# A two-block transformer kernel in fp32: the last step of four layer norms moves from GpSimd to VectorE

## The chip, the cores and the metric

The kernel runs on one core of a Trainium2 chip. Its time is the device time of one execution in microseconds; what is told is the median over runs. The engines are named as in the profile: PE is TensorE's matmul side and PEld its weight loads, DVE is VectorE, ACT is ScalarE, POOL is GpSimd, SP is SyncE, which here only issues DMAs.

## What is computed

The input is one sequence of 256 tokens of width 1024. A first block (two hybrid layers) yields `x`. The second block, in which the change lies, runs two layers over `x` (the latent stream) and a context stream `ctx` of 256 tokens:

```python
for i in range(2):
    last = i == 1
    h, hc = x * (1 + sc1) + sh1, ctx * (1 + sc1c) + sh1c
    y, yc = retention_mixer(h, hc, ...) if i == 0 else neighbourhood_mixer(h, hc, ...)
    x = layer_norm(ALPHA * x + g1 * y, ln_g[i, 0], ln_b[i, 0])
    h = x * (1 + sc2) + sh2
    x = layer_norm(ALPHA * x + g2 * sq_relu_mlp(h), ln_g[i, 1], ln_b[i, 1])
    if not last:
        ctx = layer_norm(ALPHA * ctx + g1c * yc, ln_g[i, 0], ln_b[i, 0])
        ctx = layer_norm(ALPHA * ctx + g2c * sq_relu_mlp(ctx * (1 + sc2c) + sh2c), ln_g[i, 1], ln_b[i, 1])
# sq_relu_mlp(h) = square(relu(h @ w1)) @ w2, with w1 1024 x 4096 and w2 4096 x 1024
```

## The kernel before, in words

Every engine has its own instruction list, and semaphores alone order them. All large products are made in three passes: a weight block is split by ACT into a rounded part `w_hi` (`split_hi`, L412) and by DVE into the rest `w_lo` (`split_lo`, L420), and `three` (L431 to L433) multiplies hi by hi, hi by lo and lo by hi. The weights come in units of 128x2048 fp32. SP fetches a unit into one of four `raw` slots (L368) and waits for the slot's last split; the split parts have two slots, so ACT splits unit n+2 once PE has begun unit n+1. PE takes the units in order.

Tokens lie in four tiles of 128: tiles 0 and 1 are the context (`xc`), tiles 2 and 3 the latent stream (`xs`); `x_of(t)` names tile t. `ALL` is all four, `LAT` the last two. Lines 1688 to 1724 (`dve_ahead`, `dve_half`, `dve_normal`) build ALPHA*x plus the gated result, its statistics, and the normalised tile `y`. PE transposes `y`, ACT applies the next stage's scale and shift, and DVE writes the low part `zt_lo` (L1654, semaphore `zT`), on which the next product starts. The residual stream itself is not needed for that product. It is brought up to date apart from it: `pool_gains2` loads the norm's gain and bias, broadcast over the partitions, into `gn2` (L1811; the profile calls it gn), and `pool_stream` makes x = y * gain + bias for each tile on POOL (L1819, L1822) and counts `zs_new`.

That happens three times: after the retention mixer (ALL, at the start of the first MLP), after the first MLP (ALL, at the start of the neighbourhood stage) and after the neighbourhood mixer (LAT, at the start of the second MLP). The norm after the second MLP is made in `dve_final`.

In the MLP the steps are `up` and `down` over chunks of 512 hidden columns, in the order up 0, up 1, down 0, up 2, down 1 and so on, each in two halves j of one unit. For a half of `up`, ACT makes the relu from PSUM (L2213), DVE the square (L2239, tile `hm`), ACT the rounded part `hh_hi` (L984), ACT and DVE split the next unit (L412, L420), and DVE makes `hh_lo` (L2245, semaphore `hh`). Behind the first `up` DVE waits for `zs_new` and clears `y` with one memset per tile (L2259), since `y` collects the `down` products (L1844). `gate_b` is made from `mod` (L1663) in the same stretch.

In the neighbourhood stage `nv` lies over `y` and `nq` over `gn2`, so ACT waits for `zs_new` before it writes `nv` (L984); SP waits for it before the first bias windows (`nb_windows`, L2330), and POOL before it clears `nb` (L2311).

PE has no work in the norms: `pe_keep` (L790) issues matmuls there whose results nobody reads.

Of the kernel before, what the change touches and what calls it, by code (L numbers as in the profile page):

```python
# [23 lines left out]
ALU = mybir.AluOpType  # L24
# [184 lines left out]
def build(nc, a, out):  # L209

    with ExitStack() as ctx:
        held = {}

        def on(name):
            if name not in held:
                held[name] = ctx.enter_context(nc.semaphore(name))
            return held[name]
# [83 lines left out]
        y = sc("y", [2 * NT, D])  # L301
# [1504 lines left out]
                    on("pow_out"), pool.gives("pow_out"))  # L1806

        def pool_gains2(pool, l, m):
            pool.eng.wait_ge(on("zs_new"), pool.given("zs_new"))
            for j, v in enumerate(("ln_g_2", "ln_b_2")):  # L1810
                pool.eng.dma_start(gn2[:, j, :], a[v][l, m].partition_broadcast(P)).then_inc(  # L1811
                    on("gn2_in"), pool.gives("gn2_in", 16))

        def pool_stream(pool, tiles):

            pool.eng.wait_ge(on("gn2_in"), pool.takes("gn2_in", 32))
            pool.eng.wait_ge(on("zT"), pool.takes("zT", len(tiles)))
            for t in tiles:
                G.tensor_tensor(x_of(t), y[:, t, :], gn2[:, 0, :], ALU.mult).then_inc(  # L1819
                    on("p_step"), pool.gives("p_step"))  # L1820
                pool.eng.wait_ge(on("p_step"), pool.given("p_step"))
                G.tensor_tensor(x_of(t), x_of(t), gn2[:, 1, :], ALU.add).then_inc(  # L1822
                    on("zs_new"), pool.gives("zs_new"))

        def down_unit(pe, h_hi_, h_lo_, tiles, banks, ready=None):
            hi, lo = unit_slot(pe)
# [400 lines left out]
        def dve_mlp(dve, tiles):  # L2227
            n_tok = len(tiles) * P
            streams = sorted({stream_of(t) for t in tiles})

            def step(what, b, c):
                if c is last_down:
                    return
                for j in range(2):
                    if what == "up":
                        for f in range(2):
                            dve.eng.wait_ge(on("relu"), dve.takes("relu"))
                            r2 = hm[:, 2 * j + f, 0:n_tok]
                            V.tensor_tensor(r2, r2, ps[2 * j + f][:, 0:n_tok], ALU.mult).then_inc(  # L2239
                                on("hm"), dve.gives("hm"))  # L2240
                        dve.eng.wait_ge(on("hm"), dve.given("hm"))
                        split_lo(dve)
                        for f in range(2):
                            dve.eng.wait_ge(on("hh_hi"), dve.takes("hh_hi"))
                            V.tensor_tensor(hh_lo[:, b, 2 * j + f, 0:n_tok], hm[:, 2 * j + f, 0:n_tok],  # L2245
                                                    hh_hi[:, b, 2 * j + f, 0:n_tok].bitcast(F32), ALU.subtract).then_inc(
                                                        on("hh"), dve.gives("hh"))
                    else:
                        dve.eng.wait_ge(on("y_add"), dve.given("y_add"))
                        dve_add(dve, j, tiles, down_banks(j, tiles))  # L2250
                        split_lo(dve)
                        if j == 0 and dve.loop is None:
                            dve.eng.wait_ge(on("y_add"), dve.given("y_add"))
                            dve.eng.wait_ge(on("gate_b"), dve.takes("gate_b", 2 * len(streams)))
                            dve_ahead(dve, 0, tiles)
                if what == "up" and dve.loop is None and c == 0:
                    dve.eng.wait_ge(on("zs_new"), dve.takes("zs_new", len(tiles)))
                    for t in tiles:
                        V.memset(y[:, t, :], 0.0).then_inc(on("v_step"), dve.gives("v_step"))  # L2259
                    dve.eng.wait_ge(on("v_step"), dve.given("v_step"))  # L2260

            mlp_program(dve, f"mlp{len(tiles)}", step)
            dve.eng.wait_ge(on("y_add"), dve.given("y_add"))

        def dve_final(dve):
# [2 lines left out]
            dve_half(dve, 0, 3, 5, "ahead")  # L2268
            dve_half(dve, 1, 2, 6, "added")
            dve_half(dve, 1, 3, 7, "added")  # L2270
            dve.eng.wait_ge(on("gn2_in"), dve.takes("gn2_in", 128))
            for t in LAT:
                dve.eng.wait_ge(on("pow_out"), dve.takes("pow_out"))
                o = 32 * (t % 2)
# [32 lines left out]
                nb_windows(sp, f, (2, 3))  # L2307

        def pool_nat(pool):
            pool.eng.wait_ge(on("zs_new"), pool.given("zs_new"))  # L2310
            G.memset(nb[:, 0:SEQ], 0.0).then_inc(on("p_step"), pool.gives("p_step"))  # L2311
            pool.eng.wait_ge(on("p_step"), pool.given("p_step"))
            for f in range(NF):
# [176 lines left out]
        def dve_nat(dve):  # L2490
            split_lo(dve)
            split_lo(dve)
            split_lo(dve)
            dve.eng.wait_ge(on("zs_new"), dve.takes("zs_new", len(ALL)))
            for f in range(NF):
                split_lo(dve)
                dve.eng.wait_ge(on("nqk_ps"), dve.takes("nqk_ps"))
# [92 lines left out]
        def _(eng):  # L2590
# [24 lines left out]
            for m in range(2):  # L2615
                pool_powers(pool, ALL)
                pool_gains2(pool, 0, m)
                pool_stream(pool, ALL)
            pool_nat(pool)
            pool_powers(pool, LAT)  # L2620
            pool_gains2(pool, 1, 0)
            pool_stream(pool, LAT)
            pool_gains2(pool, 1, 1)
            pool_powers(pool, LAT)

# [102 lines left out]
```

## Time and profile before

| | |
|---|---|
| median of 3 runs | 2115.38 us (2114.42 to 2117.17) |
| profiled execution, its own time | 2118.92 us |
| span of the profile | 2116.9 us |
| PE busy | 2045.9 us (97%) |
| DVE busy | 1272.1 us (60%) |
| ACT busy | 876.3 us (41%) |
| POOL busy | 184.3 us (9%) |
| mean granted clock of TensorE | 0.995 |

The busy times are of one profiled execution. The span runs from its first to its last instruction, and its own time is some 2 us longer. A busy PE is not a PE at its peak, so what matters is where PE waits, and for whom. The granted clock is 1.0 at 2.4 GHz and 0.5 at 1.2 GHz.

### The profile page before, as it was taken

Reading aid. Unit: us, or ns where it says so; the run is one execution under the profiler, and the core shown is the slowest. Engines: PE = TensorE matmul, PEld = TensorE weight load, DVE = VectorE, ACT = ScalarE, POOL = GpSimd, SP = SyncE. Lnnn points to the kernel's source line nnn. Section 1 sums busy time; section 2 is a strip of 40 time slices with the busy share of each in tenths; the row PEclk is TensorE's granted clock in tenths of the full one; section 3 lists DMA queues with packets and bytes.
Section 4 is the critical chain, followed back from the end, with each engine's and each line's share of the span. In section 5 each row is a group of like instructions: output and inputs, shape, how many; then the busy total and the mean of one; then the engine's idle time right before and its main releaser. Section 6 shows DMA issues by size and latency. Waiting matters only on the chain.

```text
span 2116.9 us, 31361 instructions
## 1 busy us (share of the span) xinstructions
PE 2045.9 (97%) x12185; PEld 1672.0 (79%) x12185; DVE 1272.1 (60%) x2047; ACT 876.3 (41%) x1459; POOL 184.3 (9%) x175
## 2 busy tenths in 40 slices
PE   8999999999999999999999999999999999789997
PEld 7776899887768998877777778788888787567996
DVE  5656677476567773744444378634445823766667
ACT  5533566354335654422222224323322433755452
POOL 2020200000200000000000004000000420302000
PEclk9999999999999999999999999999999999999999
DMA  8477665644876655322222222332333262535662
GB/s 247 160 268 250 183 178 178 193 126 159 281 256 198 175 183 165 128 79 80 64 95 59 100 60 80 100 100 85 93 99 99 80 146 86 76 93 158 187 187 85
DMA packets 327156, 297.45 MB, mean 141 GB/s; under 512 B 35030, under 2 KB 248354, under 8 KB 326928
## 3 DMA queue, kind: packets, MB, share of 16 engines
q1 hardware_dynamic: 322960, 283.22, 44.7%
q0 software_dynamic: 4096, 12.84, 1.8%
q8 instruction: 70, 1.15, 0.2%
q14 instruction: 30, 0.25, 0.0%
HBM read 294.97 MB, written 1.05 MB: 140 GB/s over the span
## 4 chain that ended last, share of the span: by engine, by line
PE 78%; DVE 13%; issue 3%; ACT 3%; DMA 1%; DVEq 0%; POOL 0%; SPq 0%; ACTq 0%; POOLq 0%
PE ps L431 22%; PE ps L433 21%; PE ps L432 21%; DVE w_lo L420 4%; PE ps L1931 2%; PE ps L499 2%; PE ps L790 1%; DVE npr L2509 1%; DVE hid L1551 1%; PE ps L696 1%; PE ps L2376 1%; PE ps L704 1%; DVE qkv L1222 1%; PE ps L706 1%; PE ps L1912 1%
## 5 line engine op out<-in xcount | busy, mean ns | idle before, releaser
L420 DVE TENSOR_TENSOR w_lo<-raw,w_hi 128x1024 fp32r<-128x1024 f32 x428 | 525.4, 1270 | 354.7 <-ACT w_hi L412 354.5
L412 ACT ACTIVATE w_hi<-raw 128x1024 fp32r<-128x1024 f32 x428 | 428.6, 1051 | 554.3 <-PE ps L431 468.1
L431 PE MATMUL ps<-zt_hi,w_hi 128*128 128x512 f32 (+1 forms) x816 | 276.6, 339 | 4.5 <-issue 1.4
L433 PE MATMUL ps<-zt_hi,w_lo 128*128 128x512 f32 (+1 forms) x816 | 274.9, 337 | 0.0
L432 PE MATMUL ps<-zt_lo,w_hi 128*128 128x512 f32 (+1 forms) x816 | 274.9, 337 | 0.0
L431 PE MATMUL ps<-xt_hi,w_hi 128*128 128x256 f32 x896 | 255.6, 285 | 12.3 <-DVE w_lo L420 10.9
L432 PE MATMUL ps<-xt_lo,w_hi 128*128 128x256 f32 x896 | 252.0, 281 | 0.0
L433 PE MATMUL ps<-xt_hi,w_lo 128*128 128x256 f32 x896 | 251.9, 281 | 0.0
L431 PEld LDWEIGHTS ps<-xt_hi,w_hi 128*128 128x128 f32 x896 | 169.6, 189 | 20.3 <-DVE w_lo L420 11.6
L431 PEld LDWEIGHTS ps<-zt_hi,w_hi 128*128 128x128 f32 x816 | 154.1, 189 | 24.9 <-issue 3.7
L432 PEld LDWEIGHTS ps<-xt_lo,w_hi 128*128 128x128 f32 x896 | 169.8, 189 | 0.0
L433 PEld LDWEIGHTS ps<-xt_hi,w_lo 128*128 128x128 f32 x896 | 169.6, 189 | 0.0
L433 PEld LDWEIGHTS ps<-zt_hi,w_lo 128*128 128x128 f32 x816 | 154.9, 190 | 18.1
L432 PEld LDWEIGHTS ps<-zt_lo,w_hi 128*128 128x128 f32 x816 | 154.1, 189 | 18.4 <-issue 0.2
L431 PE MATMUL ps<-w_hi,hh_hi 128*128 128x512 f32 x384 | 149.9, 390 | 1.7 <-DVE w_lo L420 1.7
L432 PE MATMUL ps<-w_lo,hh_hi 128*128 128x512 f32 x384 | 150.8, 393 | 0.0
L433 PE MATMUL ps<-w_hi,hh_lo 128*128 128x512 f32 x384 | 150.7, 392 | 0.0
L431 PE MATMUL ps<-w_hi,zt_hi 128*128 128x512 f32 x320 | 127.9, 400 | 1.8 <-DVE w_lo L420 1.8
L433 PE MATMUL ps<-w_hi,zt_lo 128*128 128x512 f32 x320 | 126.9, 397 | 0.0
L432 PE MATMUL ps<-w_lo,zt_hi 128*128 128x512 f32 x320 | 126.7, 396 | 0.0
L1844 DVE TENSOR_TENSOR y<-y,ps 128x512 f32<-128x512 f32 x108 | 71.9, 684 | 85.9 <-PE ps L433 85.9
L1551 DVE SCALAR_TENSOR_TENSOR hid<-ps,par,hid 128x254 f32<-128x254 f32 (+1 forms) x176 | 76.9, 478 | 59.8 <-ACT hid L1174 53.8
(382 smaller groups left out, 3424.7 us busy)
## 6 DMA issues: line engine op xcount, KB each, us to landing
raw<-in_mlp_w SPq DMA_DIRECT2D x128, 512.0 KB, 4.6
raw<-in_ada_w SPq DMA_DIRECT2D x96, 512.0 KB, 5.2
raw<-in_w_up SPq DMA_DIRECT2D x88, 512.0 KB, 5.1
raw<-in_w_in SPq DMA_DIRECT2D x56, 512.0 KB, 4.9
raw<-in_ret_w_in SPq DMA_DIRECT2D x48, 512.0 KB, 4.5
raw<-in_w_down SPq DMA_DIRECT2D x44, 512.0 KB, 4.0
raw<-in_nat_w_in SPq DMA_DIRECT2D x24, 512.0 KB, 5.0
raw<-in_w_out SPq DMA_DIRECT2D x16, 512.0 KB, 7.3
```

Source lines behind the costliest of these rows:

```text
L412: nc.scalar.activation(w_hi[:, t, w], raw[:, s, w], ACT.Copy).then_inc(on("w_hi"), act.gives("w_hi"))
L420: ins = nc.vector.tensor_tensor(w_lo[:, t, w], raw[:, s, w], w_hi[:, t, w].bitcast(F32), ALU.subtract)
L431: first = nc.tensor.matmul(out_ap, l_hi, r_hi, start=start, stop=False)
L432: nc.tensor.matmul(out_ap, l_hi, r_lo, start=False, stop=False)
L433: return first, nc.tensor.matmul(out_ap, l_lo, r_hi, start=False, stop=stop)
L499: ins = T.matmul(ps[5][32 * k:32 * k + 32, :], cs[:, 4 * j + k, 22 - 2 * g:54 - 2 * g], raw[:, s, 512 * k:512 * k + 512], start=g == j == ...
L696: ins = T.matmul(ps[2 + t][:, hs(h)], m_lev[n % 2][:, t, hs(h)], x_inv[:, t, hs(h)], start=True, stop=True)
L704: T.matmul(ps[t][:, hs(h)], xt_inv[:, t, hs(h)], dec_y[:, t, hs(h)], start=True, stop=True)
L706: ins = T.matmul(ps[2 + t][:, hs(h)], dec_y[:, t, hs(h)], xt_inv[:, t, hs(h)], start=True, stop=True)
L1551: V.scalar_tensor_tensor(dst[:, d:SEQ], src[:, 0:SEQ - d], w, dst[:, d:SEQ], ALU.mult, ALU.add).then_inc(on(sem), dve.gives(sem))
L1844: V.tensor_tensor(yt, yt, ps[banks[n]][:, :], ALU.add).then_inc(on("y_add"), dve.gives("y_add"))
L1931: ins = T.matmul(ps[4 + t][:, :], s_, rv[:, v, :], start=n == 0, stop=n == len(keys) - 1)
```

## The change

The two instructions per tile that bring the stream up to date move from POOL to DVE. In the MLPs they stand in the first `up` step, half of the tiles behind each half j; in the neighbourhood stage all four tiles stand behind DVE's second split of `dve_nat`. The products of a call come first, then one wait, then the sums. The loads of `gn2` stay on POOL, with the same condition in constants. Waits for `zs_new` on DVE become waits for its own count.

```diff
         def pool_gains2(pool, l, m):
-            pool.eng.wait_ge(on("zs_new"), pool.given("zs_new"))
+            pool.eng.wait_ge(on("zs_new"), (0, len(ALL), 2 * len(ALL), 2 * len(ALL) + len(LAT))[2 * l + m])
...
-        def pool_stream(pool, tiles):
-
-            pool.eng.wait_ge(on("gn2_in"), pool.takes("gn2_in", 32))
-            pool.eng.wait_ge(on("zT"), pool.takes("zT", len(tiles)))
+        def dve_stream(dve, tiles):
+
             for t in tiles:
-                G.tensor_tensor(x_of(t), y[:, t, :], gn2[:, 0, :], ALU.mult).then_inc(
-                    on("p_step"), pool.gives("p_step"))
-                pool.eng.wait_ge(on("p_step"), pool.given("p_step"))
-                G.tensor_tensor(x_of(t), x_of(t), gn2[:, 1, :], ALU.add).then_inc(
-                    on("zs_new"), pool.gives("zs_new"))
+                V.tensor_tensor(x_of(t), y[:, t, :], gn2[:, 0, :], ALU.mult).then_inc(
+                    on("v_step"), dve.gives("v_step"))
+            dve.eng.wait_ge(on("v_step"), dve.given("v_step"))
+            for t in tiles:
+                V.tensor_tensor(x_of(t), x_of(t), gn2[:, 1, :], ALU.add).then_inc(
+                    on("zs_new"), dve.gives("zs_new"))
...
@@ dve_mlp, behind hh_lo of half j of an up step
+                        if dve.loop is None and c == 0:
+                            if j == 0:
+                                dve.eng.wait_ge(on("gn2_in"), dve.takes("gn2_in", 32))
+                            dve_stream(dve, tiles[j * len(tiles) // 2:(j + 1) * len(tiles) // 2])
...
                 if what == "up" and dve.loop is None and c == 0:
-                    dve.eng.wait_ge(on("zs_new"), dve.takes("zs_new", len(tiles)))
+                    dve.eng.wait_ge(on("zs_new"), dve.given("zs_new"))
...
@@ dve_final
-            dve.eng.wait_ge(on("gn2_in"), dve.takes("gn2_in", 128))
+            dve.eng.wait_ge(on("gn2_in"), dve.takes("gn2_in", 32))
...
@@ pool_nat
-            pool.eng.wait_ge(on("zs_new"), pool.given("zs_new"))
+            pool.eng.wait_ge(on("zs_new"), 2 * len(ALL))
...
         def dve_nat(dve):
             split_lo(dve)
             split_lo(dve)
+            dve.eng.wait_ge(on("gn2_in"), dve.takes("gn2_in", 32))
+            dve_stream(dve, ALL)
             split_lo(dve)
-            dve.eng.wait_ge(on("zs_new"), dve.takes("zs_new", len(ALL)))
...
@@ POOL's program
             for m in range(2):
                 pool_powers(pool, ALL)
                 pool_gains2(pool, 0, m)
-                pool_stream(pool, ALL)
             pool_nat(pool)
             pool_powers(pool, LAT)
             pool_gains2(pool, 1, 0)
-            pool_stream(pool, LAT)
             pool_gains2(pool, 1, 1)
```

## Rows read from the trace of the kernel before

**Rows 1.** The page: busy time by engine, and the chain that ended last.

```profile
PE 2045.9 (97%) x12185; PEld 1672.0 (79%) x12185; DVE 1272.1 (60%) x2047; ACT 876.3 (41%) x1459; POOL 184.3 (9%) x175
PE 78%; DVE 13%; issue 3%; ACT 3%; DMA 1%; DVEq 0%; POOL 0%; SPq 0%; ACTq 0%; POOLq 0%
```

**Rows 2.** Timeline of POOL: start, length, instruction, idle before it and its releaser.

```profile
1304.26 2.40 POOL L1819 TENSOR_TENSOR xc<-y,gn 128x1024 f32<-128x1024 f32 x1 [7.44 <-DVE zt_lo L1654]
1324.87 2.71 POOL L1822 TENSOR_TENSOR xs<-xs,gn 128x1024 f32<-128x1024 f32 x1
...
1696.79 2.42 POOL L1822 TENSOR_TENSOR xs<-xs,gn 128x1024 f32<-128x1024 f32 x1
...
1931.18 2.40 POOL L1822 TENSOR_TENSOR xs<-xs,gn 128x1024 f32<-128x1024 f32 x1
```

**Rows 3.** Timeline of DVE in the first MLP's first steps, pairs merged (x2).

```profile
1317.22 5.33 DVE L420 TENSOR_TENSOR w_lo<-raw,w_hi 128x1024 fp32r<-128x1024 f32 x2 [3.12 <-ACT w_hi L412]
1322.46 5.66 DVE L2245 TENSOR_TENSOR hh_lo<-hm,hh_hi 128x512 fp32r<-128x512 f32 x2
1333.32 1.29 DVE L2245 TENSOR_TENSOR hh_lo<-hm,hh_hi 128x512 fp32r<-128x512 f32 x2
1334.77 0.91 DVE L2259 MEMSET y<- 128x1024 f32 x1 [0.16 <-issue]
...
1340.47 1.28 DVE L2239 TENSOR_TENSOR hm<-hm,ps 128x512 f32<-128x512 f32 x2 [1.57 <-ACT hm L2213]
1343.40 2.36 DVE L420 TENSOR_TENSOR w_lo<-raw,w_hi 128x1024 fp32r<-128x1024 f32 x2 [1.65 <-ACT w_hi L412]
```

**Rows 4.** Timelines of DVE, ACT and PE in the second MLP's first steps.

```profile
1931.19 4.60 DVE L420 TENSOR_TENSOR w_lo<-raw,w_hi 128x1024 fp32r<-128x1024 f32 x2 [1.97 <-ACT w_hi L412]
...
1944.04 0.75 DVE L2239 TENSOR_TENSOR hm<-hm,ps 128x256 f32<-128x256 f32 x2 [0.23 <-DVE y L2259]
1946.23 2.36 DVE L420 TENSOR_TENSOR w_lo<-raw,w_hi 128x1024 fp32r<-128x1024 f32 x2 [1.44 <-ACT w_hi L412]
...
1945.15 1.99 ACT L412 ACTIVATE w_hi<-raw 128x1024 fp32r<-128x1024 f32 x2
...
1935.85 0.39 PE L431 MATMUL ps<-zt_hi,w_hi 128*128 128x256 f32 x1 [0.59 <-DVE w_lo L420]
1948.72 0.50 PE L431 MATMUL ps<-w_hi,hh_hi 128*128 128x512 f32 x1 [1.71 <-DVE w_lo L420]
```

**Rows 5.** Timeline of PE in the first MLP: a unit's last matmul, two units' first.

```profile
1326.52 0.40 PE L433 MATMUL ps<-zt_hi,w_lo 128*128 128x512 f32 x1
1328.26 0.49 PE L431 MATMUL ps<-zt_hi,w_hi 128*128 128x512 f32 x1 [1.34 <-DVE hh_lo L2245]
...
1350.76 0.39 PE L431 MATMUL ps<-w_hi,hh_hi 128*128 128x512 f32 x1
```

**Rows 6.** The splits' line over the kernel: count, ns min/median/max, first and last start.

```profile
L420 DVE TENSOR_TENSOR w_lo<-raw,w_hi x428: 1161/1220/3466, 11.5 to 2097.0; 128x1024 fp32r<-128x1024 f32 x143
```

**Rows 7.** Timelines of DVE, ACT and PE in the neighbourhood stage's first units.

```profile
1698.68 2.75 DVE L420 TENSOR_TENSOR w_lo<-raw,w_hi 128x1024 fp32r<-128x1024 f32 x2 [4.23 <-ACT w_hi L412]
...
1699.50 2.04 ACT L984 ACTIVATE nv<-ps 128x512 f32<-128x512 f32 x4
...
1719.08 0.28 PE L431 MATMUL ps<-zt_hi,w_hi 128*128 128x256 f32 x1
```

**Rows 8.** Granted clock by stretch: length, PE busy (matmuls), clock, DMA share, GB/s.

```profile
29.00:30.00 1.00, 1.00 (x8) 0.85 1.17 291
30.00:31.00 1.00, 1.00 (x7) 0.50 1.15 288
...
33.00:34.00 1.00, 1.00 (x10) 0.95 1.06 395
```

**Rows 9.** Timeline of PE: waits elsewhere, each with its idle time.

```profile
28.84 0.38 PE L431 MATMUL ps<-xt_hi,w_hi 128*128 128x256 f32 x1 [2.67 <-DVE w_lo L420]
...
1802.94 1.14 PE L2376 MATMUL ps<-nk,nq 32*128 32x512 f32 x8 [3.36 <-DVE nsm L2509]
```

## The prediction

> **What bounds the kernel now.** I read the page first. PE is busy for 97% of the span, the chain that ended last is 78% PE and 13% DVE, and POOL has no share of it [rows 1]. So what POOL takes is worth nothing by itself. It counts only where PE waits for something behind it, and work given to DVE costs only where PE waits for DVE. I then read the timeline of POOL to find the three places where the stream is brought up to date: from 1304.26 to 1327.6, up to 1699.2, and up to 1933.6 [rows 2]. For each I read the timelines of DVE, ACT and PE side by side and looked for PE's waits and for the room that DVE's last delivery has before PE wants it. Last I read the granted clock around PE's longer gaps.
>
> Two things are to be seen. First, DVE is slow exactly while POOL works: a pair of splits takes 5.33 us at 1317 and 4.60 at 1931, where a pair takes 2.36 elsewhere, and a pair of `hh_lo` 5.66 where a pair takes 1.29 [rows 3, 4]. The Trainium skill ("SBUF — State Buffer", Who interferes with whom) has a rule for it: a VectorE instruction with two SBUF inputs and a GpSimd one that reads SBUF lock each other out of a shared port pair. These rows agree, and nothing below needs the rule. Second, the stages differ in how much room DVE has. In the first MLP two units take PE from 1328.26 to 1350.76, 11.2 us each, and DVE waits for work. In the second, with half the tokens, an `up` unit takes half of that, 5.6 us (estimate), and DVE runs nearly without a break, with PE waiting 0.59 and 1.71 us for its splits [rows 4, 5].
>
> **The change part by part.** It removes 10 pairs of POOL instructions of some 2.9 us each (eight from 1304.26 to 1327.6 [rows 2]) and puts 20 instructions of 128x1024 on DVE. The trace has none of these on DVE, so I price one by the split, the same operation with both inputs in SBUF: 1.16 to 1.22 us where nothing disturbs it [rows 6]. I take 1.21, and 0.05 for the wait between product and sum. Two tiles in one call are 4.8 us, one tile is 2.5, four are 9.7.
>
> *First MLP, gain.* The undisturbed pair of splits from 1317.22 ends at 1319.6 and `hh_lo` at 1320.9, in place of 1328.1. The gain and bias are there: POOL could start with them at 1304.26 [rows 2]. The four instructions for tiles 0 and 1 fill 1320.9 to 1325.7, and the next relu comes only when PE ends its unit, near 1327. So they are hidden. PE's wait of 1.34 us for `hh_lo` goes: the unit begins one matmul step behind 1326.52, at 1326.75, in place of 1328.26, which is 1.5 us earlier [rows 5].
>
> *First MLP, cost.* Behind the second half come tiles 2 and 3, 4.8 us, and then the four memsets of 1.07 us each with their idle piece [rows 3]. The square before this half can start some 0.5 us earlier than in the trace, since DVE is no longer held by `hh_lo`. So the first memset goes from 1334.77 to about 1339.1, the last ends at 1343.4, and the square of 1340.47 moves to 1343.4, late by 2.9. Behind it stand ACT's `hh_hi` and split and then DVE's split, which ended at 1345.76 and ends at 1348.7. PE wants that unit at 1350.76 less 1.5, at 1349.25 [rows 3, 5]. That leaves 0.6 us. The stream work costs nothing here, but the cover is almost used up: with 0.1 us more on each of the eight instructions the room would be gone. Together: -1.5, between 0 and -1.5.
>
> *Neighbourhood stage.* PE did not wait under POOL's work here, so nothing is gained. DVE's second split of `dve_nat`, begun at 1698.68, ends at 1701.0, and eight instructions take it to 1710.8. `zs_new` is then complete 11.5 us later than at 1699.2. Three engines wait for it. ACT's copies to `nv` move from 1699.50 to 1710.9 and end at 1712.9; behind them stands ACT's next split, and DVE's half of it ends at 1716.4. PE begins that unit at 1719.08 [rows 7], and everything here runs 1.5 us earlier alike, so 2.7 us are left. SP's bias windows move by 8 us, and behind them in its queue stands one fetch, late by some 7 us, of a unit that is split four units after the one begun at 1719.08. POOL's additions to the bias windows serve the scores, some 80 us later (1802.94 is one of them [rows 9]). Cost: 0, and 1 at most if DVE or ACT ran later than I read.
>
> *Second MLP.* Here DVE, ACT and DVE again form the chain. The split at 1931.19 takes 2.36 in place of 4.60, and PE's 0.59 us before 1935.85 goes. But tile 2 (2.5 us) stands before the next square, and tile 3 (2.5 us) before the two memsets. Behind them the square of 1944.04, ACT's `hh_hi` and split of 1945.15, DVE's split of 1946.23 and PE's unit at 1948.72 follow each other with no room [rows 4]. The chain to 1948.72 therefore grows by 5.0 less the 2.24 that the shorter split gives back, 2.7 to 2.8. PE begins at 1951.4 on the old scale. The half without stalls in front gives PE nothing, since it waits for the same split in the end. Behind this unit everything on DVE and ACT is shifted alike; DVE has idle pieces later, but PE, which has none, can't take time back. Cost: 2.7. The lower end is 0.5, if half of the five microseconds found idle time of DVE, the upper 5.0, if the shorter split gave nothing back.
>
> *PE's clock.* Two `up` units from 1935.85 end near 1947, so PE stands still for about 4.5 us, where it stood for 1.71. After a gap of 2.67 us the granted clock fell from 1.0 to 0.5 (2.4 to 1.2 GHz), from 29.7 to 33.1; 3.4 us of work at half rate cost 1.7 us [rows 8, 9]. After a gap of 3.36 us before 1802.94 it stayed at 1.0 [rows 9]. So the length alone does not settle it, but 4.5 is longer than either, and I take the fall as likelier than not, at 1.7. The bounds are 0 (it doesn't fall) and 3.4 (it stays down twice as long). The Trainium skill ("TensorE: Matmul & The Clock Gate", HAM oscillation — how this bites in real kernels) says that long waits of the engine throttle it again and the next products start at half rate. It speaks against this change in the same place; by it the sum would be the one given here.
>
> **Sum.** -1.5 + 0 + 2.7 + 1.7 = +2.9 us. Against the profiled execution's own time of 2118.92 that makes 2121.8. That execution lies 3.5 us above the median of the runs, and its splits and waits are the same work, so I carry the difference over: 2115.4 + 2.9 = 2118.3. A measurement of this kernel can tell about 0.2%, 4.2 us, from no change.
>
> **The rivals.**
> 1. *The clock doesn't fall.* -1.5 + 2.7 = +1.2, 2116.6. For it speaks the gap of 3.36 us without a fall; against it that the new one is longer. Chance 0.22.
> 2. *Slower: the clock stays down for two such stretches.* If it falls while PE still stands, the idle rest of the gap delays its return. -1.5 + 2.7 + up to 3.4 = +4.6, 2120.0. The one place is the unit behind the new gap, and it decides from 3.0 us at half rate's cost. For it speaks that the gap is long; nothing in the short one shows it. Chance 0.20.
> 3. *DVE's new work is hidden in the second MLP too.* The port freed from POOL is then worth all of it: PE keeps its 1.71 us and loses the 0.59, and the 1.5 come on top, -2.1, 2113.3. Against it: the chain named above has no idle piece long enough. Chance 0.06.
> 4. *Faster: the stalls go, and the half-rate stretches that PE has at the starts of the first MLP and the neighbourhood stage fall otherwise as well.* With one of them gone, -2.1 - 1.7 = -3.8, 2111.6; it would need still more to be told from no change. Chance 0.03.
> 5. *The room of 0.6 us in the first MLP or of 2.7 in the neighbourhood stage isn't there.* One more stall of 1 to 2 us makes +4 to +5, 2120. Chance 0.07.
> The forecast itself has 0.42.
>
> **How the numbers follow.** 2118.3 is the sum of the likeliest case; its own range is 2117 to 2119.5. Rival 1 reaches down to 2116.6 and the runs before spread 2.8 us, so the low end is 2115; rivals 2 and 5 lie at 2120, so the high end is 2121. Outside remain rivals 3 and 4 and the outer parts of 2 and 5, some 0.18. The bound of slower lies at 2119.6: most of rivals 2 and 5 and a tail of the forecast, 0.22. Faster by over 0.2% is 0.03, and within it 0.75.
>
> **What would show it.** In the profile after: no POOL instruction on xs or xc; splits of 2.36 a pair at 1317 and 1931; PE's wait for `hh_lo` near 1327 gone, and no wait of PE near 1349; `nv` copies near 1709 with no wait of PE behind them; in the second MLP one wait of PE for a split of 4 to 5 us in place of 1.71, and the clock at 0.5 for some 3.4 us behind it. The prediction would be wrong if DVE's instructions of the stream took far from 1.21 us, if PE waited for DVE or ACT behind the stream in the first two places, or if the new gap in the second MLP were under 3 us.

## The result: 0.2% slower

| | before | after |
|---|---|---|
| median of 20 runs each, in turn | 2117.07 us | 2120.48 us |
| lowest and highest | 2112.93 to 2122.34 us | 2116.11 to 2125.50 us |
| ratio | | 1.0020 (95%: 1.0014 to 1.0026) |

The ratio makes +4.2 us, between +3.0 and +5.5; the medians differ by 3.4. The forecast was +2.9, and 2118.3 us stood for it beside a median of 2115.38 over three runs. The 20 runs of before have a median 1.7 us higher, so the differences are what to compare. The time of after lies in the forecast's range, and the ratio lies on the bound of 0.2% that was called out of reach of a measurement. It was not: 20 pairs of runs leave an interval of 0.06% on either side.

The page of after, as [rows 1] of before. POOL has lost 57.7 us of work. DVE has 20 more instructions and is still busy for 2.0 us less.

```profile
PE 2046.3 (97%) x12185; PEld 1670.1 (79%) x12185; DVE 1270.1 (60%) x2067; ACT 876.2 (41%) x1459; POOL 126.6 (6%) x155
...
PE 79%; DVE 13%; issue 3%; ACT 3%; DMA 1%; DVEq 0%; POOL 0%; ACTq 0%; SPq 0%; POOLq 0%
...
L420 DVE TENSOR_TENSOR w_lo<-raw,w_hi 128x1024 fp32r<-128x1024 f32 x428 | 504.4, 1220 | 353.0 <-ACT w_hi L412 352.8
```

The last row says why: the 428 splits take 504.4 us at a mean of 1220 ns, the undisturbed median of [rows 6] (before: 525.4 us, mean 1270), and with what `hh_lo` lost they pay for the 20 new instructions of 1.22 us. The span, 2116.6 us, is 0.3 us under that of before [Time and profile before]; one execution can't show 3 us in it (the last section says why), so the two traces are compared place by place.

**First MLP.** The timeline of DVE in after, for [rows 3]. All times are 2.35 us earlier here than in before (the stage's first matmul stands at 1296.72, in place of 1299.07).

```profile
1314.55 2.36 DVE L420 TENSOR_TENSOR w_lo<-raw,w_hi 128x1024 fp32r<-128x1024 f32 x2 [3.12 <-ACT w_hi L412]
1316.82 1.29 DVE L2244 TENSOR_TENSOR hh_lo<-hm,hh_hi 128x512 fp32r<-128x512 f32 x2
1318.03 2.35 DVE L1817 TENSOR_TENSOR xc<-y,gn 128x1024 f32<-128x1024 f32 x2
...
1324.91 1.28 DVE L2238 TENSOR_TENSOR hm<-hm,ps 128x512 f32<-128x512 f32 x2 [2.13 <-ACT hm L2212]
...
1339.64 0.91 DVE L2262 MEMSET y<- 128x1024 f32 x1 [0.16 <-issue]
1340.78 1.29 DVE L2238 TENSOR_TENSOR hm<-hm,ps 128x512 f32<-128x512 f32 x2 [0.23 <-DVE y L2262]
1343.71 2.36 DVE L420 TENSOR_TENSOR w_lo<-raw,w_hi 128x1024 fp32r<-128x1024 f32 x2 [1.65 <-ACT w_hi L412]
```

The pair of splits takes 2.36 in place of 5.33, and `hh_lo` 1.29 in place of 5.66. The first four instructions of the stream end near 1322.8, and DVE then waits 2.13 us for the next relu: they are hidden. At 1340.78 the square has no room left; its idle piece of 1.57 us [rows 3] has become the memset's 0.23. The split that follows ends at 1346.07, and the timeline of PE shows that it is in time:

```profile
1346.48 0.40 PE L431 MATMUL ps<-w_hi,hh_hi 128*128 128x512 f32 x1
```

No row of PE in this stage has a wait for `hh_lo` any more, and the fifth unit (the first of `down`) follows without one; 0.4 us of room is left (1346.48 less 1346.07; 0.6 was expected). From the stage's first matmul to this unit it is 49.76 us, and 51.69 in before, each with 1.7 us lost to a low granted clock: 1.9 us less, where 1.5 was forecast.

**Neighbourhood stage.** The timelines of DVE and ACT, for [rows 7]:

```profile
1694.34 2.36 DVE L420 TENSOR_TENSOR w_lo<-raw,w_hi 128x1024 fp32r<-128x1024 f32 x2 [8.62 <-ACT w_hi L412]
...
1703.55 2.35 DVE L1821 TENSOR_TENSOR xs<-xs,gn 128x1024 f32<-128x1024 f32 x2
1708.98 2.36 DVE L420 TENSOR_TENSOR w_lo<-raw,w_hi 128x1024 fp32r<-128x1024 f32 x2 [3.08 <-ACT w_hi L412]
...
1705.94 2.07 ACT L984 ACTIVATE nv<-ps 128x512 f32<-128x512 f32 x4 [10.68 <-DVE xs L1821]
...
1714.73 0.28 PE L431 MATMUL ps<-zt_hi,w_hi 128*128 128x256 f32 x1
```

ACT stands for 10.68 us before `nv`, and the split behind it ends at 1711.3. PE begins that unit at 1714.73 without a wait, so 3.4 us of room are left (2.7 expected). SP's bias windows come 6.5 us later after the stage's first matmul than in before, and the fetch behind them 3.8 us later (8 and 7 expected); PE waits for neither.

**Second MLP.** The timelines of DVE and PE, for [rows 4]:

```profile
1928.15 2.36 DVE L420 TENSOR_TENSOR w_lo<-raw,w_hi 128x1024 fp32r<-128x1024 f32 x2 [1.96 <-ACT w_hi L412]
1930.43 0.75 DVE L2244 TENSOR_TENSOR hh_lo<-hm,hh_hi 128x256 fp32r<-128x256 f32 x2
1931.10 1.22 DVE L1817 TENSOR_TENSOR xs<-y,gn 128x1024 f32<-128x1024 f32 x1
...
1933.50 0.74 DVE L2238 TENSOR_TENSOR hm<-hm,ps 128x256 f32<-128x256 f32 x2
...
1938.69 1.22 DVE L1817 TENSOR_TENSOR xs<-y,gn 128x1024 f32<-128x1024 f32 x1
...
1941.45 0.91 DVE L2262 MEMSET y<- 128x1024 f32 x1 [0.28 <-DVE xs L1821]
1943.66 0.75 DVE L2238 TENSOR_TENSOR hm<-hm,ps 128x256 f32<-128x256 f32 x2 [0.23 <-DVE y L2262]
1945.84 2.36 DVE L420 TENSOR_TENSOR w_lo<-raw,w_hi 128x1024 fp32r<-128x1024 f32 x2 [1.43 <-ACT w_hi L412]
...
1948.33 0.49 PE L431 MATMUL ps<-w_hi,hh_hi 128*128 128x512 f32 x1 [4.44 <-DVE w_lo L420]
```

From 1928.15 to the split of 1945.84 DVE never waits longer than 1.5 us, and both of those waits (1.50 and 1.43) are for ACT's split, which itself waits for DVE's square. PE waits once, 4.44 us, where it waited 0.59 and 1.71. From the stage's first matmul to this one it is 29.06 us (1919.27 to 1948.33), and 26.62 before (1922.10 to 1948.72): +2.44, where +2.7 was forecast.

The granted clock behind the gap, in stretches of 2 us (length, PE busy and matmuls, clock, DMA share, GB/s):

```profile
1948.00:1950.00 2.00, 1.67 (x6) 0.79 0.11 11
1950.00:1952.00 2.00, 2.00 (x6) 0.50 0.93 309
1952.00:1954.00 2.00, 2.00 (x9) 0.85 0.54 208
```

It fell to 0.5 when PE had just started again, and stayed there for 3.4 us (1949.2 to 1952.6 in stretches of 0.2 us): 1.7 us lost. The Trainium skill ("TensorE: Matmul & The Clock Gate", HAM oscillation — how this bites in real kernels) says the same: half rate after a long wait. This trace agrees: 4.44 us of wait, then 3.4 us at 0.5.

### The profile page after: what moved, and what is told of

The parts are those of the page before. It is cut to its first block, busy times and chain, and to the rows that moved or that the text cites. A ratio compares the mean times of both kernels' runs of the same rounds, so it can differ in the third digit from the quotient of the medians.

```text
span 2116.6 us, 31357 instructions
## 1 busy us (share of the span) xinstructions
PE 2046.3 (97%) x12185; PEld 1670.1 (79%) x12185; DVE 1270.1 (60%) x2067; ACT 876.2 (41%) x1459; POOL 126.6 (6%) x155
## 4 chain that ended last, share of the span: by engine, by line
PE 79%; DVE 13%; issue 3%; ACT 3%; DMA 1%; DVEq 0%; POOL 0%; ACTq 0%; SPq 0%; POOLq 0%
PE ps L431 22%; PE ps L432 21%; PE ps L433 21%; DVE w_lo L420 4%; PE ps L1930 2%; PE ps L499 2%; DVE npr L2513 1%; PE ps L790 1%; DVE hid L1551 1%; PE ps L2379 1%; PE ps L696 1%; PE ps L704 1%; DVE qkv L1222 1%; PE ps L706 1%; PE ps L1911 1%
## 5 line engine op out<-in xcount | busy, mean ns | idle before, releaser
L420 DVE TENSOR_TENSOR w_lo<-raw,w_hi 128x1024 fp32r<-128x1024 f32 x428 | 504.4, 1220 | 353.0 <-ACT w_hi L412 352.8
```

The lines of the kernel that those rows point to most:

```text
L420: ins = nc.vector.tensor_tensor(w_lo[:, t, w], raw[:, s, w], w_hi[:, t, w].bitcast(F32), ALU.subtract)
```

## The experiments

Each kernel was run on one chip together with before, in five rounds (double_again in four). Ratios are to before on the same chip, with their 95% interval; most reach 0.1% (2 us) to either side, so that one ratio alone settles little and pairs of kernels on one chip count. Where DVE's part is changed, its waits for `gn2_in` and `zs_new` are written in constants, and where a part stays on POOL, `pool_stream` stands there as in before, with its waits in constants too.

### One place at a time

`after_same` is the changed kernel again. `lat_on_pool` gives only the second MLP's part back to POOL, `lat_only` has only this part on DVE, `first_only` only the first MLP's, `nat_only` only the neighbourhood stage's. `on_pool_again` and `first_again` are `lat_on_pool` and `first_only` once more.

```diff
@@ lat_on_pool; the others in the same way
-                        if dve.loop is None and c == 0:
+                        if dve.loop is None and c == 0 and len(tiles) == 4:
...
             pool_gains2(pool, 1, 0)
+            pool_stream(pool, LAT, 3)
             pool_gains2(pool, 1, 1)
```

> The changed kernel again, as the common measure for the kernels that share its chip. By my reading (first MLP -1.5 us, second MLP's chain +2.7, PE's clock behind its longer gap +1.7) 2 to 5 us above the kernel before. In the trace PE waits 4.4 us for a split in the second MLP's first chunk and the granted clock is 0.5 for some 3.4 us behind it. If the clock's fall there was a chance of the one execution profiled so far, it is missing in this one.

> The changed kernel with the second MLP's two tiles given back to POOL; the first MLP's and the neighbourhood stage's stay on DVE. Theory A (the whole loss is the DVE, ACT, DVE chain of the second MLP and the clock behind its gap): 1 to 2 us below the kernel before, and 4 us below the changed kernel; PE's wait there is 1.7 us again, and the clock stays at 1.0. Rival B (work on DVE costs wherever it is put, and the loss is spread over the three places): still 1 to 3 us above the kernel before.

> The kernel before with only the second MLP's two tiles moved to DVE. Theory A: the whole loss without the first MLP's gain, +4 to +5 us against the kernel before, 1.5 above the changed kernel; PE waits 1.34 us for hh_lo in the first MLP as before, and 4.4 us in the second, with the clock at 0.5 behind it. Rival B: a fifth of the instructions, so below +1 us.

> The kernel before with only the first MLP's four tiles moved to DVE. Theory A: PE's wait for hh_lo is gone, no new one behind it, -1.5 us against the kernel before, and the neighbourhood stage's part is worth nothing, so it equals lat_on_pool, whose ratio was 0.9986. Rival D (part of that gain came from the neighbourhood stage): above lat_on_pool by the difference.

> The kernel before with only the neighbourhood stage's four tiles moved to DVE. Both theories: 0 within what can be told (below 1 us either way). In the trace ACT's first copies to nv come 6 to 7 us later and the unit behind them starts without a wait of PE; the waits in both MLPs are those of the kernel before.

> The same kernel as lat_on_pool, on one chip with first_again, so that the neighbourhood stage's part is their difference. Theory A: 1 to 3 us below the kernel before, within 1 us of first_again. Rival D (the neighbourhood stage's part gains 2 us, which the two chips so far would allow): 2 us below first_again. Rival E (it costs 1.5 us, which nat_only alone would allow): 1.5 above first_again.

> The same kernel as first_only: only the first MLP's tiles on DVE, 1 to 2 us below the kernel before.

| kernel | before, this (medians) | ratio | chip |
|---|---|---|---|
| after_same | 2118.38, 2120.66 | 1.0013 (1.0003 to 1.0022) | 14 |
| lat_on_pool | 2118.38, 2115.22 | 0.9986 (0.9978 to 0.9995) | 14 |
| lat_only | 2118.38, 2121.34 | 1.0017 (1.0007 to 1.0027) | 14 |
| first_only | 2117.17, 2114.83 | 0.9996 (0.9987 to 1.0006) | 2 |
| nat_only | 2115.75, 2116.47 | 1.0007 (0.9998 to 1.0017) | 5 |
| on_pool_again | 2116.90, 2116.04 | 0.9993 (0.9983 to 1.0003) | 5 |
| first_again | 2116.90, 2116.08 | 0.9998 (0.9989 to 1.0007) | 5 |

The second MLP's part alone makes the kernel as slow as the whole change does, and the whole change without it is no slower than before; on chip 14 it is faster. Its size comes from three comparisons on one chip each: after_same less lat_on_pool, 0.0027; lat_only less before, 0.0017; and ctrl_again (below; its order of work is that of after) less on_pool_again, 0.0020. They make 5.7, 3.6 and 4.2 us, mean 4.5, each good to some 2 us. The forecast had 2.7 + 1.7 = 4.4. In the profile of lat_on_pool PE's wait at this place is the old one:

```profile
1951.57 0.50 PE L431 MATMUL ps<-w_hi,hh_hi 128*128 128x512 f32 x1 [1.70 <-DVE w_lo L420]
```

The first MLP's part alone is worth -0.8 and -0.4 us by its two ratios, where -1.5 was forecast. Both intervals reach below -2, so the ratios don't refute the forecast. The profile of lat_only, where POOL does this part, shows one way in which it can be less:

```profile
1327.02 0.49 PE L431 MATMUL ps<-zt_hi,w_hi 128*128 128x512 f32 x1 [0.66 <-DVE hh_lo L2255]
```

The wait that the change removes is 0.66 us here (0.62 in nat_only) and was 1.34 in the profile of before [rows 5]: the same instructions on POOL and DVE hold each other up by a different amount from one kernel or execution to the next. The traces give the size better than the ratios do. From the stage's first matmul to its fifth unit, less what a low clock took there, it is 49.98, 49.47 and 49.43 us in the three profiles with this work on POOL, and 48.02 to 48.56, mean 48.25, in the fourteen with it on DVE and nothing added. That is a gain of 1.2 us against lat_only and nat_only and 1.7 against before.

The neighbourhood part came out at 1.0007 alone, between -0.4 and +3.6 us, and on chip 5 (second time) the first MLP's part and this one together are at 0.9993, beside 0.9998 for the first alone. The two disagree in sign and neither excludes zero. The timeline of ACT in nat_only shows the same wait as in after, and no wait of PE at any place behind it:

```profile
1703.57 2.06 ACT L984 ACTIVATE nv<-ps 128x512 f32<-128x512 f32 x4 [10.69 <-DVE xs L1832]
```

### Is each chain closed, and where does the room end?

In `lat_double` DVE makes the product and the sum of tile 3 a second time behind the second half of the second MLP. In `first_double` and `double_again`, which are the same kernel, it makes those of tiles 2 and 3 a second time in the first MLP. The product is made anew from `y` each time, so the stream's values stay the same.

```diff
@@ lat_double, behind hh_lo of half j = 1
+                            if len(tiles) == 2 and j == 1:
+                                for _ in range(1):
+                                    dve_extra(dve, tiles[1:2])
                             dve_stream(dve, tiles[j * len(tiles) // 2:(j + 1) * len(tiles) // 2])
@@ first_double and double_again
                             dve_stream(dve, tiles[j * len(tiles) // 2:(j + 1) * len(tiles) // 2])
+                            if len(tiles) == 4 and j == 1:
+                                dve.eng.wait_ge(on("zs_new"), dve.given("zs_new"))
+                                for _ in range(1):
+                                    dve_extra(dve, tiles[2:4])
```

> The changed kernel with product and sum of tile 3 made twice behind the second half of the second MLP's first up step, two more instructions of 1.22 us in the chain; the numbers come out the same. Theory A (closed chain, no idle time in it): PE's wait grows from 4.4 to 6.8 or 6.9 us, one for one, and the time by 2.4 us or a little more where the clock stays low longer. Rival (idle time of DVE takes them up): the wait grows by less than half of that.

> The changed kernel with products and sums of tiles 2 and 3 made twice behind the second half of the first MLP's first up step, four more instructions, 4.75 us; the numbers come out the same. Theory A (the room there is nearly used up, 0.3 to 0.4 us left by the changed kernel's trace): PE gets a new wait of 4.2 to 4.5 us for the split of its fifth unit, near 1346 us, and the time goes 4 us above the changed kernel, 5 to 6 with the clock behind the gap. Rival (the first MLP has room enough for DVE's extra work, since its units are twice as long): the changed kernel's time.

> The same kernel as first_double, whose profiled execution fell under a throttle over its whole length and can't be read by place. Its times (1.0056) lie 8 us above the changed kernel's, where I expected 4 to 6. Theory A: one new wait of 4.2 to 4.5 us near 1346 us, 1.7 to 3.4 us of half rate behind it, and nothing else new. Rival F (the second half's doubled work also delays the half behind it): a second new wait of 1 us or more within the next units.

lat_double: 2124.08 beside 2117.17 on chip 2, 1.0034 (1.0021 to 1.0047). Two more instructions of 1.22 us took the stretch from the stage's first matmul to its fifth unit from 29.06 to 31.57 us, +2.51, and PE's wait from 4.44 to

```profile
1952.26 0.79 PE L431 MATMUL ps<-w_hi,hh_hi 128*128 128x512 f32 x1 [6.77 <-DVE w_lo L420]
```

So what is put on DVE here reaches PE in full: the chain is closed.

first_double: 2128.30 beside 2115.75 on chip 5, 1.0056 (1.0043 to 1.0069). Its profiled execution had a granted clock of 0.75 from start to end and a span of 2527.1 us, so its waits don't compare with the others'; double_again is there for its trace. double_again: 2126.29 beside 2117.18 on chip 9, 1.0039 (1.0027 to 1.0051), and its timeline of PE has a new wait where the room was:

```profile
1355.53 0.50 PE L431 MATMUL ps<-w_hi,hh_hi 128*128 128x512 f32 x1 [4.35 <-DVE w_lo L420]
```

Four instructions, 4.78 us, brought 4.35 us of wait: the room was 0.4 us, as read off the trace of after. Behind the wait the clock was at 0.5 for 3.4 us (1.7 us lost), and up to 1440 PE has no second new wait, so the rival with two is refuted. The trace thus gives 6.1 us over after. The times give 4.0 by this kernel's ratio less the 1.0020 of after, and 7.6 by that of first_double, where 5 to 6 was expected.

### What the clock costs

If matmuls that nobody reads fill PE's gap, the clock should stay up while DVE's chain stays as it is. For this PE's program of the second MLP is written out instead of looped (`clock_ctrl`, and again `ctrl_again`), so that the filler stands only in the first `down`; `clock_keep` has 8 calls of it and `keep_half` 4.

```diff
@@ clock_ctrl, ctrl_again, clock_keep, keep_half
+            if key == "mlp2" and lane.name == "tensor":
+                for _ in range(MLP_TURNS):
+                    run(turn, 0)
...
@@ clock_keep (keep_half: pe_keep(7, 4))
+                if what == "down" and len(tiles) == 2 and c == 0:
+                    pe_keep(7, 8)
                 for j in range(2):
```

> The changed kernel with TensorE's loop over the second MLP's chunks written out, so that something can be put into its first turn alone; the same matmuls in the same order. Both theories: as the changed kernel, 2 to 5 us above the kernel before, with PE's wait of 4.4 us and the clock at 0.5 behind it.

> As clock_ctrl, with eight matmuls that nobody reads (128x512, some 3.7 us by the ones in the norms) put into PE's 4.4 us gap. The wait for the split stays, and PE's next unit starts at the same moment. Theory A (the gap also costs by the clock): the granted clock stays at 1.0 behind the gap and the time is 1.5 to 2 us below clock_ctrl. Rival C (the half-rate stretch comes there by chance or costs nothing, as DVE is the bound in this stage): no difference.

> As clock_keep, with half of the filling matmuls. In clock_keep they took 7.03 us instead of the 3.7 that I had expected and ran 2.1 us past the split that the unit behind them waits for; half of them is 3.5 us, inside the gap of 4.4. Theory A (the gap costs by the clock too): the unit starts 29.0 us after the stage's first, as in clock_ctrl, the clock stays at 1.0, and the time is 1.2 to 1.7 us below the loop written out alone. Rival C: no difference from it.

> The same kernel as clock_ctrl, on the chip of keep_half, for that comparison: 3 to 4.5 us above the kernel before, the clock at 0.5 behind the gap.

| kernel | before, this (medians) | ratio | chip |
|---|---|---|---|
| clock_ctrl | 2117.17, 2121.27 | 1.0017 (1.0008 to 1.0026) | 2 |
| clock_keep | 2117.17, 2120.06 | 1.0013 (1.0004 to 1.0023) | 2 |
| ctrl_again | 2116.90, 2119.45 | 1.0013 (1.0004 to 1.0022) | 5 |
| keep_half | 2116.90, 2117.22 | 1.0005 (0.9996 to 1.0014) | 5 |

clock_keep had too much filler. A call is two instructions of 0.44 us, 16 in all, and PE's next unit began only at 1950.45, 2.2 us after the split had ended (1948.21). The clock stayed at 1.0, and in spite of a fifth unit that began 31.18 us after the stage's start, not 29.01, the kernel was no slower than its control; the 1.5 to 2 us that it was to gain didn't come (0.8 by the ratios, and the noise is larger). keep_half removes this flaw: its filler ends before the split, and the timeline of PE has

```profile
1943.38 3.60 PE L790 MATMUL ps<-cst 128*128 128x512 f32 x8
1947.85 0.50 PE L431 MATMUL ps<-w_hi,hh_hi 128*128 128x512 f32 x1 [0.88 <-DVE w_lo L420]
```

Its chain is as long as the control's (29.21 and 29.20 us from the first matmul to the fifth unit). The clock behind the gap, first of keep_half, then of ctrl_again:

```profile
1949.00:1951.00 2.00, 2.00 (x11) 1.00 0.78 232
...
1951.00:1953.00 2.00, 2.00 (x6) 0.50 0.71 238
```

So the difference is the clock's alone: 2.2 us by the medians, 1.7 by the ratios, and between 0.9 and 3.0 by the two sets of eleven runs.

The kernels with this gap let the clock be read seven times over: after, after_same, lat_only, lat_double, double_again (whose second MLP is that of after), clock_ctrl and ctrl_again have PE stand for 4.11 to 6.77 us, and in all seven the clock fell. In the eleven other profiles that can be read (before is one) PE stands there for at most 1.71 us, and it fell in none. How long it stayed down differs. In after and after_same it fell when PE ran again and was back 3.4 us later. In the other five it fell while PE still stood, and was back only 6.8 us later. The clock of lat_only, by stretches of 1 us, whose fifth unit begins at 1950.32:

```profile
1948.00:1949.00 1.00, 0.00 (x0) 0.70 0.14 53
1949.00:1950.00 1.00, 0.00 (x0) 0.50 0.00 0
...
1954.00:1955.00 1.00, 1.00 (x4) 0.50 0.98 379
1955.00:1956.00 1.00, 1.00 (x5) 0.89 0.10 39
```

The first 2 us of its low stretch cost nothing, since PE stands; the rest costs 2.5. The time lost in the seven (one less the clock, times PE's busy time, added up) is 1.7 twice and 2.4 to 2.6 five times, mean 2.3. From the fifth unit to the end of the span the seven take 168.71 us in the mean and the eleven 167.24, so 1.5 of the 2.3 show in the span; this remainder differs by 2.2 us within the eleven alone.

### The same work in DVE's idle pieces

If the loss is the place and not the engine, the change can be kept without it. `holes` moves the second MLP's part to where DVE waits: both products and the sum of tile 2 behind the last split of the neighbourhood stage, the sum of tile 3 and the two memsets into the idle pieces around the squares. `holes_sums` leaves the memsets in their old place; `holes_again` is `holes` once more.

```diff
@@ the end of dve_nat
             split_lo(dve)
+            dve.eng.wait_ge(on("gn2_in"), 96)
+            for t in LAT:
+                V.tensor_tensor(x_of(t), y[:, t, :], gn2[:, 0, :], ALU.mult).then_inc(
+                    on("v_step"), dve.gives("v_step"))
+            dve.eng.wait_ge(on("v_step"), dve.given("v_step"))
+            V.tensor_tensor(x_of(2), x_of(2), gn2[:, 1, :], ALU.add).then_inc(on("zs_new"), dve.gives("zs_new"))
@@ dve_mlp, between the squares and split_lo; early: the second MLP's first up
+                        if early and j == 0:
+                            V.tensor_tensor(x_of(3), x_of(3), gn2[:, 1, :], ALU.add).then_inc(
+                                on("zs_new"), dve.gives("zs_new"))
+                        if early and j == 1:
+                            V.memset(y[:, 3, :], 0.0).then_inc(on("v_step"), dve.gives("v_step"))
                         split_lo(dve)
...
+                        if early and j == 0:
+                            V.memset(y[:, 2, :], 0.0).then_inc(on("v_step"), dve.gives("v_step"))
```

> The changed kernel with the second MLP's stream work put into pieces in which DVE stood idle: both products and the first sum behind the split that ends before the first square (4 us idle), the second sum between the first square and its split (2 us idle), and the two memsets one behind hh_lo of the first half and one between the second square and its split. The same instructions on the same engine. Theory A (what costs is the place in the chain, not the work): PE waits for no split there, the clock stays at 1.0, and the time is 3 to 4.5 us below the kernel before, 6 to 8 below the changed one. Rival B (DVE has too much to do in this stage wherever it stands): PE still waits 2 us or more there, and the time is not below the kernel before.

> As holes, but the two memsets of the second MLP stand where they stood, behind hh_lo of the second half. Theory A: the stream is out of the chain and the memsets (2.1 us) are in it, so PE waits some 1.5 us for the split before its third unit, as the kernel before does, its 0.59 us wait is gone, and the time lies 1.5 to 2.5 us above holes and 2 to 3 below the kernel before. Rival B: as holes, since the chain had other room.

> The same kernel as holes, on the chip of these runs, for the comparison with holes_sums: 3 to 5 us below the kernel before, no wait of PE for a split in the second MLP's first chunk.

holes: 2113.68 beside 2118.38 on chip 14, 0.9979 (0.9969 to 0.9989). holes_again: 2113.67 beside 2115.75 on chip 5, 0.9991 (0.9982 to 1.0000). holes_sums: 2116.56 beside 2115.75, 1.0004 (0.9995 to 1.0013). holes_again gains less than the 3 to 5 us expected, and holes_sums nothing where 2 to 3 was expected. The timelines of DVE and PE in holes:

```profile
1922.25 2.35 DVE L2579 TENSOR_TENSOR xs<-y,gn 128x1024 f32<-128x1024 f32 x2
1924.64 1.23 DVE L2582 TENSOR_TENSOR xs<-xs,gn 128x1024 f32<-128x1024 f32 x1
1926.29 0.75 DVE L2238 TENSOR_TENSOR hm<-hm,ps 128x256 f32<-128x256 f32 x2 [0.42 <-ACT hm L2212]
1927.08 1.23 DVE L2243 TENSOR_TENSOR xs<-xs,gn 128x1024 f32<-128x1024 f32 x1
1928.93 2.36 DVE L420 TENSOR_TENSOR w_lo<-raw,w_hi 128x1024 fp32r<-128x1024 f32 x2 [0.63 <-ACT w_hi L412]
...
1944.42 0.40 PE L431 MATMUL ps<-w_hi,hh_hi 128*128 128x512 f32 x1
```

The four instructions fill pieces in which DVE waited 3.95 and 1.96 us for ACT in after; what is left of them is 0.42 and 0.63. PE has no wait before its fifth unit, which begins 24.30 us after the stage's first matmul, 4.76 earlier than in after and 2.32 earlier than in before. The same instructions on the same engine, in other places, are worth 7 us against after_same by the medians of chip 14 (2120.66 and 2113.68), and the 4.76 with the clock's 1.7 to 2.5 account for them.

Not all of this belongs to the stream: holes also moves the two memsets, which stood in the chain of before as well. holes_sums tells the two apart. The timeline of PE there:

```profile
1944.74 0.49 PE L431 MATMUL ps<-w_hi,hh_hi 128*128 128x512 f32 x1 [1.49 <-DVE w_lo L420]
```

Its fifth unit begins 25.96 us after the stage's first matmul (1918.78). So 3.1 of the 4.76 come from the four instructions of the stream and 1.7 from the memsets, and holes_sums is 2.9 us above holes_again by the medians (1.5 to 2.5 expected). Its eleven runs have a mean clock of 0.9945 beside 0.9952 in holes_again, so part of that is clock, though no low stretch stands at this place in its profile. holes has the lowest medians of the study, clearly below before on chip 14 and just below it on chip 5. But it is not clear of lat_on_pool (2113.68 and 2115.22 on chip 14), and the kernel before with only its memsets moved was not tried.

## Why the prediction came out as it did

*The reading of the bound* held. POOL lost 57.7 us and nothing came of it but what PE had waited for.

*First MLP, gain.* The wait of 1.34 us went, DVE's instructions took 1.21 to 1.23 us (1.21 forecast), the memsets and the square fell where they were put. Whether it was worth 1.5 us is less sure: the wait is 0.62 to 0.66 us in two other profiles with the same work on POOL, the traces make the gain 1.2 to 1.7, and first_only and first_again measured -0.8 and -0.4.

*First MLP, cost, and neighbourhood stage.* No new wait; the room of 0.6 is 0.4, measured twice, the room of 2.7 is 3.4, and ACT's wait before `nv` cost PE nothing in the trace.

*Second MLP.* Right in place, mechanism and size: +2.44 us for 2.7 (+2.6 between the means of six profiles with this work on POOL and six with it on DVE), a gap of 4.44 for 4.5. Both halves of the argument stand: lat_double shows that the chain passes on what is put into it, holes and holes_sums that outside it PE does not wait for the stream.

*The clock* is the term that was mis-sized, and the first step that failed. The clock fell, as taken; rival 1 didn't occur in any of seven profiles. But the 1.7 was one low stretch of 3.4 us after the start of the kernel [rows 8], and the seven lost 2.3 in the mean. The mean clocks of whole runs say the same: 0.9942 over the 20 runs of after and 0.9953 over the 141 runs of before that stood beside the experiments, which is some 2.2 us. What rival 2 says, that a clock which falls while PE still stands returns later, is what five of them show. Only its price was too high: its "up to 3.4" counts a whole doubled stretch, and part of that stretch is idle, so 2.4 to 2.6 came out, and its deciding point of 3.0 was never reached. Rivals 3 and 5 are refuted by the waits in after, rival 4 by the sign.

*The sum.* The terms as measured: +2.4 for the chain, +2.3 for the clock, -1.2 to -1.7 for the first MLP, 0 for the neighbourhood stage, together +3.0 to +3.5. The interval of the result, +4.2 (3.0 to 5.5), covers that. The clock's term was too small by 0.6, for one reason: it was the reading of one low stretch in one execution. PE's wait of 1.34 us for `hh_lo` was such a reading too, though the runs leave open whether its term was off. The time itself was counted from 2115.4, the median of three runs, and 20 runs put it 1.7 us higher: against that, the 2118.3 of the forecast is only 1.2 above before, and the measured medians differ by 3.4. The 0.7 to 1.2 us between the terms and the +4.2 are within its interval and not assigned. Whether the neighbourhood part costs anything stays open (-0.4 to +3.6 us alone, the other sign in the second comparison), and so does whether the true ratio is above or below 1.0020: the three other kernels with the changed kernel's order of work gave 1.0013, 1.0017 and 1.0013, +2.8 to +3.6 us.

*How the numbers follow* is the second step that failed. From a sum of +2.9, 1.3 us under the bound of 0.2% and with terms of 1 us uncertainty, it made "no change" at 0.75, and gave 0.22 to what lies above the bound. The kernel is slower, clear of noise, by a ratio of 1.0020 (1.0014 to 1.0026). And nearly every uncertain term leaned upward: the clock could stay down longer, the gain in the first MLP could be smaller, its room was 0.6 us; only a clock that didn't fall could lower the sum. Nor is 4.2 us the least that a measurement can tell: 20 pairs of runs tell 1.3. Only rivals 3 and 4, with 0.09 between them, had the other sign, and the chances of slower and of no change should have stood near each other.

## What to carry to other kernels

Moving work off a slow engine pays only where the bounding engine waits for it, and the receiving engine charges for it where it is a link of a closed chain: read the receiver's waits in the trace, ask who releases them, and put the moved instructions into those that no later link depends on. Here the places of four such instructions and two memsets were worth 7 us. A wait of PE that grows to the size of those here (the clock fell in all seven of 4.1 us or more) must be costed with the clock behind it, and a gain that comes from two engines disturbing each other is not to be taken at the size of one execution.

## What the runs showed of the hardware

What POOL's two-input instructions cost DVE is not a constant. The longest split of before took 3466 ns [rows 6], the longest of after 1228. But a pair of splits that took 5.33 us in before took 4.63 in lat_only and 4.58 in nat_only, with the same work on POOL, and PE's wait behind such a pair and `hh_lo` was 1.34 us once and 0.66 and 0.62 there.

The same wait can leave the clock up or not. PE waits 3.36 us for `nsm` in both kernels; in before the clock behind it [rows 9] stayed at 1.00 (first row), and in after, where the products behind it begin at 1798.69, it was at half:

```profile
1803.00:1804.00 1.00, 1.00 (x8) 1.00 0.63 85
...
1799.00:1800.00 1.00, 1.00 (x8) 0.50 0.62 78
...
1802.00:1803.00 1.00, 1.00 (x10) 0.80 0.01 2
```

At the start of the neighbourhood stage it is the other way round, with the two lengths met behind the new gap. In before the clock fell at 1671.5, while PE stood before the unit of 1672.14, and was back at 1678.3; in after it fell at 1669.3, behind the start of the same unit at 1669.09, and was back near 1672.7. The clock of before in that stretch, by 2 us:

```profile
1672.00:1674.00 2.00, 1.85 (x4) 0.50 0.98 313
1674.00:1676.00 2.00, 2.00 (x6) 0.50 1.04 321
1676.00:1678.00 2.00, 2.00 (x6) 0.50 0.98 257
```

So of one and the same gap the clock takes 1.7 us or some 3, by where in it it falls.

Such stretches come and go between executions of one kernel, each worth 1.7 us or more, and the clocks on record show that they make most of the spread. In the 20 runs of after the mean granted clock goes from 0.992 to 0.996, and a thousandth less goes with 2.2 us more time (correlation -0.94). In the 141 runs of before on five occasions it is 1.8 us (-0.73): 2120.5 us in the mean of the 26 runs at 0.994, 2117.3 at 0.995 (68 runs), 2114.6 at 0.997 (18 runs). This is why two spans 0.3 us apart say nothing of a change of 4.
